# A decoder layer with routed experts: the small expert tiles' gate products ahead of their up products, in two PSUM banks, and three transposes put behind another

## The reference

```python
for e in range(N_EXPERTS):                      # 16
    h = jax.nn.silu(t @ w_gate[e]) * (t @ w_up[e])   # 1024 -> 512
    y = y + combine[:, e:e + 1] * (h @ w_down[e])    # 512 -> 1024
```

## Time and profile before

| | |
|---|---|
| median of three runs | 904.09 us (903.54 to 906.26) |
| the profiled execution | 903.4 us, of which 901.6 us are the span of the profile |
| mean granted TensorE clock | 0.987 |
| PE busy | 846.9 us, 94% of the span |
| DVE, ACT, POOL busy | 623.8, 572.3 and 239.4 us |
| expert stage in the profile | from about 500 us to the end |

### The profile page before, as it was taken

The page is one execution under the profiler, slowest core; times in us unless marked ns, Lnnn a source line. Parts: engine busy times, 40 slices in busy tenths (PEclk is TensorE's granted clock), DMA queues, the critical chain, the costliest instruction groups (busy, mean ns, idle before and its releaser), DMA issues.

```text
span 901.6 us, 19323 instructions
## 1 busy us (share of the span) xinstructions
PE 846.9 (94%) x5860; PEld 675.8 (75%) x5861; DVE 623.8 (69%) x1290; ACT 572.3 (63%) x1030; POOL 239.4 (27%) x421
## 2 busy tenths in 40 slices
PE   6999999999999989999987989998989999999993
PEld 4888888888888867788876756775768787777782
DVE  3866666666766677444579847883849799977991
ACT  3765564647474757222240858895869899888980
POOL 4101101010102010000032252535344454445450
PEclk9999999999999998999999999999999999999997
DMA  9801010101000162354482887876699999989963
GB/s 328 271 26 47 1 48 0 47 0 47 23 23 23 48 187 72 142 184 161 143 308 85 315 268 247 306 273 182 231 309 349 304 385 391 363 299 358 391 253 47
DMA packets 54736, 168.71 MB, mean 187 GB/s; under 512 B 9584, under 2 KB 11952, under 8 KB 54704
## 3 DMA queue, kind: packets, MB, share of 16 engines
q1 hardware_dynamic: 47312, 143.12, 43.1%
q0 software_dynamic: 7376, 25.18, 10.7%
q10 hardware_dynamic: 16, 0.01, 0.0%
HBM read 144.54 MB, written 23.75 MB: 187 GB/s over the span
## 4 chain that ended last, share of the span: by engine, by line
PE 54%; issue 17%; ACT 8%; DMA 6%; POOL 5%; DVE 5%; POOLq 2%; SPq 1%; ACTq 1%; DVEq 1%
PE bank_j L1091 10%; PE bank_j L1093 9%; PE bank_j L1092 9%; PE bank_j L1157 6%; ACT w_high L711 4%; PE bank_j L1163 3%; DMA PT<-in_w_in_dram 3%; POOL tick L605 2%; PE bank_t L1229 2%; PE bank_o L1235 2%; POOL hn L642 1%; PE bank_t L1085 1%; PE bank_s L1221 1%; POOLq L653 1%; POOL out_dram L647 1%
## 5 line engine op out<-in xcount | busy, mean ns | idle before, releaser
L1091 PE MATMUL bank_j<-w_high,rows_high 128*128 128x512 f32 x512 | 207.1, 404 | 0.6 <-DVE rows_low L2186 0.6
L1093 PE MATMUL bank_j<-w_high,rows_low 128*128 128x512 f32 x512 | 200.6, 392 | 0.0
L1092 PE MATMUL bank_j<-w_low,rows_high 128*128 128x512 f32 x512 | 200.5, 392 | 0.0
L605 POOL TENSOR_TENSOR tick<-mhalf 1x1 f32<-1x1 f32 x192 | 82.9, 440 | 187.1 <-DVE lg L2199 72.7
L2087 DVE TENSOR_TENSOR w_low<-w_res,w_high 128x1024 fp32r<-128x1024 f32 x96 | 114.3, 1220 | 6.9 <-ACT w_high L711 6.9
L1091 PEld LDWEIGHTS bank_j<-w_high,rows_high 128*128 128x128 f32 x512 | 96.6, 189 | 28.4 <-issue 7.4
L1093 PEld LDWEIGHTS bank_j<-w_high,rows_low 128*128 128x128 f32 x512 | 96.5, 189 | 21.0
L1092 PEld LDWEIGHTS bank_j<-w_low,rows_high 128*128 128x128 f32 x512 | 96.9, 189 | 18.2 <-issue 0.2
L711 ACT ACTIVATE w_high<-w_res 128x1024 fp32r<-128x1024 f32 x96 | 97.6, 1050 | 0.0
L1157 PE MATMUL bank_j<-hnT,w_res 128*128 128x128 f32 x512 | 60.3, 276 | 0.0
L1157 PEld LDWEIGHTS bank_j<-hnT,w_res 128*128 128x128 f32 x512 | 58.4, 192 | 0.9
(11 more groups left out here) (392 smaller groups left out, 1826.0 us busy)
## 6 DMA issues: line engine op xcount, KB each, us to landing
w_res<-in_w_gate_dram SPq DMA_DIRECT2D x48, 512.0 KB, 6.8
w_res<-in_w_up_dram SPq DMA_DIRECT2D x48, 512.0 KB, 7.5
bias<-in_w_down_dram SPq DMA_DIRECT2D x32, 512.0 KB, 7.4
slot_b<-in_w_gate_dram SPq DMA_DIRECT2D x16, 512.0 KB, 10.4
PT<-in_w_up_dram SPq DMA_DIRECT2D x16, 512.0 KB, 10.5
gmix<-in_w_down_dram SPq DMA_DIRECT2D x16, 512.0 KB, 7.0
h<-in_w_down_dram SPq DMA_DIRECT2D x16, 512.0 KB
hn<-in_x_dram SPq DMA_DIRECT2D x8, 512.0 KB, 3.4
```

Source lines behind the costliest of these rows:

```text
L605: pool.tensor_tensor(tick[:, len(ticks):len(ticks) + 1], mhalf[0:1, 0:1], mhalf[0:1, 0:1], ALU.mult)
L1091: pe.matmul(out_, ah, bh, start=start, stop=False)
L1092: pe.matmul(out_, ah, bl, start=False, stop=False)
L1093: return pe.matmul(out_, al, bh, start=False, stop=stop)
```

## The change

In small tiles only. PE computes all gate products (64 records of 128 columns) into `J0` and then all up products (64 of 128 columns) into `J1`. `pe_gup` is raised once after the gate products, and then once with each of the four pairs of up chunks; before, it was raised by two after the first pair of chunks and by one after each of the others. ACT's silu waits for the first of these counts, and DVE's product for all five, besides the silu. Of the eight transposes of the next rows, five stay ahead of the transpose of the inner rows and three are put behind it. The waits of `rows_T` stay in front of the first transpose.

```diff
@@ ACT
             def small_tile(t, h):
                 act.activation(warm[:, 0:1], warm[:, 1:2], ACT.Silu)
-                act.wait_ge(pe_gup, (FC + 1) * (t + 2))
+                act.wait_ge(pe_gup, (FC + 1) * (t + 1) + 1)
@@ PE
-            raw_both = [wres[:, 2 * j * PW:2 * (j + 1) * PW].rearrange("p (g k n) -> p g k n", g=2, k=2) for j in range(3)]
 
             def small_tile(t, e):
                 pe.wait_ge(act_raw, t + 1)
                 wait(pe, dve_mh, 2 * t)
 
-                for k in range(KC):
-                    j, kk = k // 2, k % 2
-                    if kk == 0:
-                        for i in (k, k + 1):
-                            pe.wait_ge(ld_piece[i], e * 16 + landed[i])
-                    for g in range(1 if j < 3 else 2):
+                for g, bank in enumerate((J0, J1)):
+                    for k in range(KC):
+                        j, kk = k // 2, k % 2
+                        if kk == 0:
+                            pe.wait_ge(ld_piece[2 * j + g], e * 16 + landed[2 * j + g])
                         for q in range(4):
                             at, cols = slice(q * QP, (q + 1) * QP), slice(q * P, (q + 1) * P)
-                            out_ = J0[at, 0:2 * P] if j < 3 else J0[at, g * P:(g + 1) * P]
-                            b = raw_both[j][:, :, kk, cols] if j < 3 else raw_gu[j][g][:, kk, cols]
-                            ins = pe.matmul(out_, raw_rows[:, k, 0:QP], b, start=(k == 0), stop=(k == KC - 1),
-                                            skip_group_check=True)
-                    if kk == 1:
-                        ins.then_inc(pe_gup, 2 if k == 1 else 1)
-                rows_T(t + 1)
-                pe.wait_ge(dve_mh, 2 * t + 1)
-                wait(pe, dve_hT, 2 * t)
-                pe.transpose(S0[:, 0:P], mh[:, 0:P], ident[:, :]).then_inc(pe_hT, 1)
+                            ins = pe.matmul(bank[at, 0:P], raw_rows[:, k, 0:QP], raw_gu[j][g][:, kk, cols],
+                                            start=(k == 0), stop=(k == KC - 1), skip_group_check=True)
+                        if g == 1 and kk == 1:
+                            ins.then_inc(pe_gup, 1)
+                    if g == 0:
+                        ins.then_inc(pe_gup, 1)
+                pe.wait_ge(ld_g, 16 * (t + 2))
+                pe.wait_ge(dve_mx, 2 * t + 2)
+                pe.wait_ge(act_raw, t + 1)
+                for k in range(KC):
+                    if k == 5:
+                        pe.wait_ge(dve_mh, 2 * t + 1)
+                        wait(pe, dve_hT, 2 * t)
+                        pe.transpose(S0[:, 0:P], mh[:, 0:P], ident[:, :]).then_inc(pe_hT, 1)
+                    ins = pe.transpose(bank_t[:, k * P:(k + 1) * P], xg[:, k * P:(k + 1) * P], ident[:, :])
+                ins.then_inc(pe_mx, 1)
                 wait(pe, y_ready, 2 * t)
@@ DVE
             def small_tile(t, h):
                 dve.wait_ge(act_silu, 2 * t + 2)
+                dve.wait_ge(pe_gup, (FC + 1) * (t + 2))
                 wait(dve, pe_hT, 2 * t)
-                dve.tensor_tensor(mh[:, 0:P], sg[:, 0:P], J0[:, P:2 * P], ALU.mult).then_inc(dve_mh, 1)
+                dve.tensor_tensor(mh[:, 0:P], sg[:, 0:P], J1[:, 0:P], ALU.mult).then_inc(dve_mh, 1)
```

## The result

The kernel after took 912.56 us, the median of nine runs (910.73 to 917.65); the kernel before took 904.51 us beside it (nine runs, 903.00 to 909.51). The ratio is 1.0091 [1.0075, 1.0107]. The forecast was 903.1 with a range to 906.0, and a gain of 1.0 us; measured were a loss of 8.1 us and a time 9.5 us above the forecast. The profiled execution took 912.48 us with a span of 910.7: 9.1 us more than the span of before, 901.6.

What follows compares the result with a forecast made beforehand. TensorE's work was taken to make over half of the time, the rest many short handovers. Gains of 0.66 us in following tiles and 0.3 from scatters, rounded 1.0, gave 903.1 us against a median of 904.09; range 900.0 to 906.0.

Steps and rivals of the forecast that it cites:

- The products: PE's gate and up products in small tiles: 128 short records take 3.49 us, as the mixed ones did; cost 0.
- the rival of the short matmuls: Small tiles: short matmuls don't keep their pace; at 1.3 us more a tile, 910.0 us; chance 0.06.
- the three signs by which the forecast was to be known as wrong: First tiles shorter, a full tile's transposes waiting for a gather, or waits for inner rows vanishing at the two held places.
- The weight loads: Next expert's loads start about 1.3 us later, which frees the scatters of two held tiles; gain 0.3 us for both together.
- gets there earlier and waits longer: Experts with two small tiles: PE, held by the scatter's landing, turns their 0.35 us each into waiting in the full tile.
- the rival of the clock: Two full tiles: longer PE waits for inner rows drop the clock once or twice, 1.1 us each; 905.4 us; chance 0.12.
- The three late transposes fit under that.: First small tiles: three transposes, 0.33 us, fit in the 0.91 us between the inner rows' transpose and down products.
- The four following tiles: Small tiles behind another: 0.35 and 0.31 us gained in the expert with three, together 0.66; other two gain only the scatter's.
- The silu in the eight first tiles: Small tiles first in their expert: silu moves over a microsecond ahead, but PE still waits for DVE; gain 0.
- The rival that they get shorter: First small tiles: DVE isn't the limit, so 12 x 0.35 + 0.3 = 4.5 us come off, 899.6; chance 0.07.
- The next rows and the gathers: After small tiles: rows copies end about 0.15 us later, gathers shift at most 1.3 us within 1.5 of cover; cost 0.
- The rival that the scatters land near 3.5 us: Experts with two small tiles: the later loads free the scatters and stalls go; 3.7 us gained, 900.4; chance 0.08.

Runs made afterwards that it cites:

- experiment 1: Also after_short_last: kernel after, with the last expert's never-executed small tile in its form of before on PE, ACT and DVE; 906.58 us, ratio 1.0016.
- experiment 3: Also before_pad48: kernel before, with 48 extra matmuls in the last expert's small tile, which isn't run; 911.18 us, ratio 1.0063.
- experiment 4: Also after_shifted: kernel after, with 12 filler matmuls ahead of the expert stage left out, moving the branch down 48 instructions; 908.26 us, ratio 1.0029.
- before_pad24: Kernel before, with 24 extra matmuls in the last expert's small tile, which isn't run; 905.26 us, ratio 1.0004.
- before_split53: Also experiment 5: kernel before, with only the transposes split five and three around the inner rows' transpose; 905.03 us, ratio 1.0011.
- experiment 6: Also after_products_only: kernel after, but all eight transposes ahead and the last expert's small tile in its form of before; 906.56 us, ratio 1.0014.
- experiment 7: Kernel before, but SP waits for all of a small tile's products ahead of every gate and up piece; 906.46 us, ratio 1.0002.
- experiment 9: Kernel before, but SP loads gate and up pieces only after the last small tile's down products; 903.47 us, ratio 0.9977.
- experiments 9 to 11: Loads held until the last small tile's down products: kernel before 903.47 us; kernel after, last expert's small tile as before, 900.27; same, half of them done, 900.39.
- after_gate_early: Kernel after, last expert's small tile in its form of before, gate pieces loaded once the gate products are done; 906.78 us, ratio 1.0012.

## Why the prediction was wrong, point by point

**The products, "I cost it at 0".** This is the step that failed. As execution it was right: 128 short records keep the pace of 32, and the rival of the short matmuls, whose 910.0 is near the result, is refuted by its own sign, 27 to 28 ns in every small tile. The 1.2 us a tile that the prediction estimated from the Trainium skill, TensorEngine Tiling (Array Packing), Performance Considerations, did not come: 3.63 us from start to transposes against 3.60. The same section says that a matmul over 1 column has the latency of one over 60, so its 60 cycles can be meant as a floor and not as an addition; with 128 columns in each matmul these runs speak only against the addition. But the step priced instructions only where they run. It never asked what 96 more of them do to the program's layout. Added in the loop, and again in a copy that isn't executed, they moved the landing place of a taken branch from 17.34 blocks to 18.08. That cost a 5 us gap and, since PE's clock fell to half 0.2 us after it went on, 1.6 us in the last tile: 6.6 us by the traces, 6 by the medians of experiment 1, and 5.7 by the ratio of experiment 3. The Trainium skill, Runtime: NRT & Kernel Launch, Instruction fetch mechanics, says that a taken branch to code outside the two blocks at hand has to fetch it before execution goes on; by that rule, a branch whose target has moved ahead had to be counted, and the traces agree with it. I did not weigh it. The section gives no price; here that is 4.5 to 5.2 us for the gap.

That it is the code, and neither the order of the products nor DVE, is shown: experiment 1 removes the gap without touching anything that runs, experiment 3 makes it in the kernel before, experiment 4 removes it by moving the same branch. That the edge lies at the border of a block is argued from the counts and that section, not seen in a trace. None of the three signs by which the forecast was to be known as wrong came up: they all looked at stretches that the change touches.

**The weight loads, "I take 0.3 us for both places".** The shift was right, 1.3 us, and the sign of its effect was wrong. The two scatters landed after 7.5 and 7.8 us instead of 6.9 and 7.4. That holds over the traces: with the loads of before (before, before_pad24, before_pad48, before_split53) they took 6.5 to 7.0 and 6.8 to 7.4 us, with those of after (after, after_short_last, after_shifted, after_products_only) 7.1 to 7.5 and 7.5 to 7.8. The row of 6.9 from which I drew the rule lies in a third place, where the loads start almost with the scatter; there a later start did shorten the scatter, by 1.8 us (experiment 7), but ACT had waited only 0.85 us for it. At the held places the loads stay ahead of the scatter, and the same shift goes the other way. The clause that went with it, PE "gets there earlier and waits longer", came true, and with it the rival of the clock (0.12), at one of its two places and above its price of 1.1: the products and transposes of 676.6 to 680.9 us took 1.6 us longer. That the longer scatters cost time is another matter, and isn't shown: in before_pad24 and before_pad48, whose code that runs is that of before, these experts took 39.92 and 37.54, and 38.59 and 38.59 us, more together than the 37.52 and 39.20 of after. What is left of the loss without the gap is +1.4 and +1.3 us by the ratios of experiments 1 and 6, with intervals from about none to 2.6, and how it divides between the scatters, the first tiles and chance stays open.

**"The three late transposes fit under that."** They don't quite: from the transpose to the down products it is 0.10 us more in each of the eight first tiles, and experiment 5 puts it down to them. The five that are their expert's only small tile get longer by it, 0.57 us in all; the three that a second one follows don't (8.10 us before and 8.09 after in the expert with three). ACT's copy follows the transpose by 0.50 us as before; what grew is from the copy to the down products, 0.51 us (584.51 to 585.02) instead of 0.40 (583.64 to 584.04 in the earlier trace rows). Why a wait after three transposes ends later than one after none was not tried.

**The four following tiles, 0.66 us.** Right: 8.85 + 7.74 before, 8.35 + 7.50 after, 0.74 with a gather that landed 0.2 us sooner. Experiments 5 and 6 add that neither half brings it alone.

**The silu in the eight first tiles, 0.** Right, and by the reason given: 4.75 us from start to transpose in both kernels. The rival that they get shorter is out. **The next rows and the gathers, 0.** Right: no full tile's transposes came to wait for a gather.

**The rival that the scatters land near 3.5 us** had about the right size for what was there to be had (3.7 us forecast, 4.9 measured over both experts in experiment 9), and the wrong road: at the held places 1.3 us later isn't enough. The scatter lands after 3.4 to 3.6 us where the loads start 7.7 to 9.1 us after the tile instead of 1.3 (experiments 9 to 11).

## What to carry to other kernels

Count a change's instructions also where they don't run: code inside a skipped branch shifts and lengthens jumps, and one that comes to land two 16 KB blocks ahead cost 5 us here, at an instruction that no line of the change touches; a gap whose named releaser was long done, with one code transfer in it and another right behind, is the mark. Where a small scatter shares the engines with megabytes of loads, a small shift of the loads can lengthen the scatter or shorten it, depending on which of the two starts first, but holding them back until the scatter is through can be worth several microseconds. And a change that makes an engine early at a place where something else decides has bought a longer wait, perhaps with half a clock behind it.

## What the runs showed that I had not expected

- The code gap has a sharp edge: targets at up to 17.90 blocks by the count of the table cost nothing, targets at 18.08 and 18.09 cost 4.5 to 5.2 us, all with branches that start in block 16. Which blocks are held, and what a branch from early in a block to late in the next would do, stays open.
- A small scatter takes 3.4 to 3.6 us with no load beside it and up to 8.5 beside loads. At the place of the earlier trace rows it took 7.4 us with the first load 1.3 us after the tile's start, 7.8 with 2.6 and 8.1 with 3.9; at the other held place 6.9, 7.5 and 7.1, so the order is not strict; in the expert with three it took 6.9, 5.1 and 3.5.
- How long PE stood still doesn't decide by itself whether the granted clock falls: in the kernel after it fell to half once PE had gone on after 2.55 and after 4.83 us, and stayed up after 2.50 us; in after_gate_early it fell after 1.84 us and stayed up after 2.69. In the kernel after it was back within 4 us of PE's restart, both times.
